# A two-layer trunk on one core: small parameters laid out by partition and loaded in three transfers, the weight queue started without them

## The chip, the cores and the metric

One NeuronCore of one Trainium2 chip. The metric is the device time of one execution in microseconds; of several runs the median is taken. Times in the rows are microseconds from the start of one profiled execution, unless marked ns.

## What is computed

The reference runs two layers on x (256 tokens, 1024 channels, float32), modulated by a vector c. Cut to what matters here:

```python
c_act = silu(c)
for i in range(2):
    mod = c_act @ ada_w[i] + ada_b[i]                  # 6144 numbers: shift, scale, gate, twice
    h = rmsnorm(x, norm_g[i, 0]) * (1 + scale_m) + shift_m
    y = s5_mixer(h, ...) if i == 0 else stick_breaking_attention(h, ...)
    x = x + gate_m * rmsnorm(y, norm_g[i, 1])
    h = rmsnorm(x, norm_g[i, 2]) * (1 + scale_f) + shift_f
    y = swiglu(h, ...) if i == 0 else moe_swiglu(h, ...)   # 8 experts, top 2
    x = x + gate_f * rmsnorm(y, norm_g[i, 3])

# s5_mixer, per group of 16 channels with a complex state of 64:
u = h @ w_in; step = exp(log_step)
lb = exp((lam_re + i lam_im) * step)                   # decay of the state
bb = (lb - 1) / lam * (b_re + i b_im)
state = scan(lb, bb u); y = re((c_re + i c_im) state) + d_skip * u
out = split(gelu(y) @ w_out): val * sigmoid(gate)
```

## The kernel before

The program is written out by hand for each engine, in one block; engines meet at semaphores only. Big weights (`ada_w`, `s5_w_in`, `s5_w_out`, the feed-forward and expert weights) come in pieces of 2 MB, 128 partitions by 4096 float32, into a ring of seven buffers. SP issues all of them (`load`, L532) in a fixed order of places: place n lies in buffer n mod 7, a load waits until the product on the buffer's last content has counted up `used`, and its landing counts up `landed`. The first places are four pieces of `ada_w[0]` (0 to 3), `s5_w_in` (4), four more of `ada_w[0]` (7 to 10), and the two halves of `s5_w_out` (11, 12). Buffers 5 and 6 hold `bs` and `wv`, small matrices that the kernel makes for the S5 layer, until places 12 and 13. At the start SP waits for `params_in` to reach 16 times 13 (L543), which is the landing of 13 parameter transfers; after that it issues pieces 0 and 1, piece 2 behind the landing of 0, piece 3 behind that of 1, and `s5_w_in` behind that of 2 (L544 to L549).

ACT's queue issues everything small (L724 to L739): c, both lambdas, log_step, d, norm_g and ada_b as rows (7 transfers), x (1 MB), the four parts of b, the two of c_re and c_im (4 and 2 transfers, with runs of 64 and 256 bytes), then the router's weights and bias. Only behind these 16 issues do ACT's own instructions follow: the squares of x (`pre_stats`, L748), Silu of c (L842), two sines, four copies of blocks of the identity (L847), four evictions of the transposed c (L853), then the evictions of the modulation (`ada_part` L779, `ada_mod` L784) and of `wv` (L793), and a part of hT (L757).

DVE waits for the 13 transfers (L1495), spreads log_step (L1496), and lets PE transpose the rows into columns (L2222, 17 transposes, and 32 matmuls for c_re and c_im, L2287). It copies them out of PSUM (L1498, L1499) and begins a long chain of small instructions on 128 x 16 elements, each waiting for the one before: `exp_small` (L1369 to L1380), c32, which is Silu(c) repeated for the product (L1505), angles, `to_hT` (x times its inverse norm, L1386), powers of the decay, then `bs` in four wide steps (L1483 to L1487, `complex_blocks`), `hT_evict` (L1394), the tables of angles (L1454 to L1463), and `resp`.

PE waits for c32 and for pieces 0 and 1 for the first product (`ada(0)`, L2248, 32 matmuls), transposes x (L2267), folds (L2258), does `ada(1)` on pieces 2 and 3, folds, transposes `bs` in eight groups (L2304, groups 4 to 7 need the second half of `bs`), and then needs hT for u (L2312). After that come the chunk sums (L2334), responses, `ada(2)`, `ada(3)`, outputs (L2371, L2373), the product with `s5_w_out` (L2413), and the later layers.

GpSimd (POOL) makes the constants, sets buffer 5 to zero (L695), waits for the squares of x and makes the two inverse norms (`inverse_norm`, L655 and L656), sets `resp` (5120 columns) to zero (L697), marks buffers 5 and 6 as landed (L699), and adds `ada_b` to the modulation (`mod_bias`, L662 to L670), on which hT waits.

Of the kernel before, what the change touches and what calls it, by code (L numbers as in the profile page):

```python
# [31 lines left out]
ACT = mybir.ActivationFunctionType  # L32
AX = mybir.AxisListType

P = 128
D = 1024
KD = D // P
# [3 lines left out]
NBLK = W5 // P  # L41
HG = 16
NS = 64
TPB = 4
NT = NBLK * TPB
# [4 lines left out]
NE = 8  # L50
# [81 lines left out]

def ada_place(layer, r):

    return ADA_PLACES[layer][r]
# [7 lines left out]
def program(nc, x, c, ada_w, ada_b, norm_g, s5_w_in, s5_lambda_re, s5_lambda_im, s5_b_re, s5_b_im,  # L143
            s5_c_re, s5_c_im, s5_d, s5_log_step, s5_w_out, sb_w_qkv, sb_w_out, ffn_w_gate_up,
            ffn_w_down, moe_w_router, moe_b_router, moe_w_gate_up, moe_w_down, out):
    ctx = ExitStack()
    with ctx:
        def sb(name, shape, dt=F32):
            return ctx.enter_context(nc.sbuf_tensor(name, shape, dt))

        def sem(name):
            return ctx.enter_context(nc.semaphore(name))

        ps = ctx.enter_context(nc.psum_tensor("ps", [P, 8, 512], F32))
# [4 lines left out]
        ident = sb("ident", [P, P])  # L159
# [6 lines left out]
        cols = sb("cols", [P, 128])  # L166
        c32 = sb("c32", [P, KD, 32])
        adab = sb("adab", [P, 4, 24])
# [4 lines left out]
        wr_sb = sb("wr_sb", [P, KD, NE])  # L173
# [61 lines left out]
        c_raw = view(at_u, (2, NBLK, NS))  # L235
        b_raw = view(at_u + 2 * NBLK * NS, (2, NT, HG))
# [59 lines left out]
        params_in, x_in, router_in = sem("params_in"), sem("x_in"), sem("router_in")  # L296
        out_written, consts_done = sem("out_written"), sem("consts_done")
        cols_ready, cols_ps, cols_done, silu_c_done, gg_done = (
            sem("cols_ready"), sem("cols_ps"), sem("cols_done"), sem("silu_c_done"), sem("gg_done"))
# [10 lines left out]
        ct_ps, ct_done, bs_done, bt_ps, wv_done = (  # L310
            sem("ct_ps"), sem("ct_done"), sem("bs_done"), sem("bt_ps"), sem("wv_done"))
# [35 lines left out]
        r_c = rows[0:KD, 0:P]  # L347
        r_lam = rows[0:NT, 128:384].rearrange("p (a n) -> p a n", a=2)
        r_ls = rows[0:NT, 384:386]
        r_lsb = rows[0:NT, 512:640].rearrange("p (a n) -> p a n", a=2)  # L350
        r_d = junk[0:NBLK, 512:640]
        r_g = tbuf[0:8, :]
        r_b = junk[0:24, 0:512]
# [6 lines left out]

        C_C, C_LRE, C_LIM, C_LS, C_D, C_G = 0, 8, 24, 40, 56, 60
# [168 lines left out]
        def _(sp):  # L530
# [12 lines left out]
            sp.wait_ge(params_in, 16 * 13)  # L543
# [80 lines left out]
        def _(pool):  # L624
# [47 lines left out]
            def router_lanes():  # L672

                pool.wait_ge(router_in, 32)
# [20 lines left out]
            pool.memset(ring[:, RING - 2, :], 0.0).then_inc(blank_done, 1)  # L695
            inverse_norm(0, ss_done, rs_done, 0, 8)
            pool.memset(resp.rearrange("p i t d h -> p (i t d h)"), 0.0).then_inc(blank_done, 1)  # L697
# [25 lines left out]
        def _(act):  # L723
            act.dma_start(r_c, c.rearrange("a (k n) -> (a k) n", n=P)).then_inc(params_in, 16)  # L724
            act.dma_start(r_lam[:, 0, :], s5_lambda_re[0].rearrange("(t g) n -> t (g n)", g=2)).then_inc(params_in, 16)
            act.dma_start(r_lam[:, 1, :], s5_lambda_im[0].rearrange("(t g) n -> t (g n)", g=2)).then_inc(params_in, 16)
            act.dma_start(r_ls, s5_log_step[0].rearrange("(t g) -> t g", g=2)).then_inc(params_in, 16)
            act.dma_start(r_d, s5_d[0].rearrange("(b g) h -> b (g h)", b=NBLK)).then_inc(params_in, 16)
            act.dma_start(r_g, norm_g.rearrange("a b n -> (a b) n")).then_inc(params_in, 16)
            act.dma_start(r_b, ada_b.rearrange("l (r n) -> (l r) n", n=512)).then_inc(params_in, 16)  # L730
            act.dma_start(x_sb[:, :, :], x[0].rearrange("(t p) d -> p t d", p=P)).then_inc(x_in, 16)
            for i, w in enumerate((s5_b_re, s5_b_im)):
                for g in range(2):
                    act.dma_start(b_raw[NS * g:NS * g + NS, i], w[0].rearrange("(t g) n h -> g n t h", g=2)[g]
                                  ).then_inc(params_in, 16)
            for i, w in enumerate((s5_c_re, s5_c_im)):
                act.dma_start(c_raw[:, i], w[0].rearrange("(b g) h n -> (g h) b n", b=NBLK)).then_inc(params_in, 16)
            act.dma_start(wr_sb[:, :, :], moe_w_router[0].rearrange("(k p) n -> p k n", p=P)).then_inc(router_in, 16)
# [100 lines left out]

            pre_stats(0)  # L840
            act.wait_ge(cols_done, 1)
            act.activation(cols[:, 0:KD], cols[:, 0:KD], ACT.Silu).then_inc(silu_c_done, 1)  # L842
# [5 lines left out]
            act.wait_ge(ct_ps, 1)  # L848
            for i in range(2):
                c_t = ps[:, 2 + i, :].rearrange("p (t g h) -> p t g h", g=2, h=HG)  # L850
                for g in range(2):
                    r = slice(NS * g, NS * g + NS)
                    act.activation(cT[r, i], c_t[r, :, g, :], ACT.Copy, scale=-1.0 if i else 1.0).then_inc(ct_done, 1)  # L853
# [495 lines left out]
        def _(dve):  # L1349
            count = [0]  # L1350

            def link(ins):

                count[0] += 1
                ins.then_inc(dve_step, 1)
                dve.wait_ge(dve_step, count[0])
# [148 lines left out]
            dve.tensor_copy(c32[:, :, :], cols[:, 0:KD].unsqueeze(2).to_broadcast([P, KD, 32])).then_inc(cols_done, 1)  # L1505
# [56 lines left out]
            dve.wait_ge(blank_done, 1)  # L1562
            complex_blocks(lambda i: bs[:, i], bs_done, (QR, QI),
# [656 lines left out]
        def _(pe):  # L2220
            def columns(dst, src, n):
                return pe.transpose(dst, src, ident[0:n, 0:n])  # L2222
# [4 lines left out]
            columns(ps[:, 0, C_LRE:C_LRE + NT], r_lam[:, 0, :], NT)  # L2227
            columns(ps[:, 0, C_LIM:C_LIM + NT], r_lam[:, 1, :], NT)
            columns(ps[:, 0, C_LS:C_LS + NT], rows[0:NT, 512:640], NT)
            columns(ps[:, 0, C_D:C_D + NBLK], r_d, NBLK)  # L2230
            for k in range(KD):
                ins = columns(ps[:, 0, C_G + 8 * k:C_G + 8 * k + 8], r_g[:, P * k:P * k + P], 8)
            ins.then_inc(cols_ps, 1)
            for j in range(4):
                ins = columns(ps[:, 1, 24 * j:24 * j + 24], r_b[:, P * j:P * j + P], 24)
            ins.then_inc(cols_ps, 1)
# [47 lines left out]
            for i in range(2):  # L2284
                for b in range(NBLK):
                    for g in range(2):
# [977 lines left out]
_INS = ["x", "c", "ada_w", "ada_b", "norm_g", "s5_w_in", "s5_lambda_re", "s5_lambda_im", "s5_b_re", "s5_b_im",  # L3264
        "s5_c_re", "s5_c_im", "s5_d", "s5_log_step", "s5_w_out", "sb_w_qkv", "sb_w_out", "ffn_w_gate_up",
        "ffn_w_down", "moe_w_router", "moe_b_router", "moe_w_gate_up", "moe_w_down"]
# [17 lines left out]
```

## Time and profile before

| What | Value |
|---|---|
| Median of 3 runs | 1480.8 us (1478.76 to 1483.89) |
| Profiled execution, its own time | 1483.81 us |
| Its span in the trace | 1482.0 us |
| Busy: PE / DVE / ACT / POOL | 1338.5 / 661.2 / 514.1 / 41.1 us |
| Moved by DMA | 474.30 MB, 320 GB/s on the mean |
| Mean granted clock of PE | 0.969 |

The span is what the trace covers; the time of the execution holds 1.8 us more. PE is busy for 90% of the span, but that is a mean over stages with different limits. In the views below "idle before <- releaser" is the time for which an engine stood before an instruction and what ended it; PEclk is the granted clock as a share of 2.4 GHz; the DMA share is the mean share of time for which the 16 DMA engines were occupied. The queue q1 holds SP's transfers, q10 ACT's.

### The profile page before, as it was taken

The page shows a single profiled execution, that of the slowest core. Times are in us where ns is not written, and L with a number is a line of the kernel's source. Part 1 is how long each engine was busy: PE and PEld are TensorE (multiplying, and loading weights), DVE is VectorE, ACT ScalarE, POOL GpSimd, SP SyncE. Part 2 cuts the span into 40 slices and gives each one's busy share as a digit, 9 for nine tenths or more (in the row PEclk, how much of TensorE's full clock was granted, in tenths as well). Part 3 has the DMA queues.
Part 4 walks back from the last instruction along what each step waited for, and adds up shares of the span by engine and source line. Part 5 has one row for each costly group of instructions (what it writes and reads, how often), then busy time and mean ns, then how long its engine had stood idle before and what let it go on. Part 6 is the DMA issues. An engine that isn't in the chain of part 4 may idle for free.

```text
span 1482.0 us, 25306 instructions
## 1 busy us (share of the span) xinstructions
PE 1338.5 (90%) x11159; PEld 956.7 (65%) x11160; DVE 661.2 (45%) x741; ACT 514.1 (35%) x563; POOL 41.1 (3%) x80
## 2 busy tenths in 40 slices
PE   3899899999999898999999999999988888987776
PEld 2674578888779645677775777776766665643332
DVE  5953354454453525555553755553864544000002
ACT  2323433434254514344442444443544441000001
POOL 3000000000010003000000000000000000000000
PEclk8989999999999998999999999999999999999999
DMA  8874794555484314799999989999999999999994
GB/s 283 331 283 153 286 412 172 179 206 183 170 341 171 114 57 170 285 341 387 412 411 412 389 335 380 410 412 412 411 411 410 409 412 412 409 413 412 412 412 181
DMA packets 206792, 474.30 MB, mean 320 GB/s; under 512 B 9986, under 2 KB 10030, under 8 KB 206670
## 3 DMA queue, kind: packets, MB, share of 16 engines
q1 hardware_dynamic: 199968, 470.83, 82.1%
q10 hardware_dynamic: 6702, 1.71, 0.5%
q8 instruction: 93, 1.52, 0.4%
q14 instruction: 29, 0.24, 0.0%
HBM read 471.47 MB, written 1.05 MB: 319 GB/s over the span
## 4 chain that ended last, share of the span: by engine, by line
PE 66%; SPq 14%; DMA 13%; DVE 3%; ACT 2%; issue 1%; ACTq 1%; POOL 1%; POOLq 0%; DVEq 0%
PE ps L2437 39%; SPq L534 14%; DMA ring<-in_moe_w_down_dram 9%; PE ps L2768 6%; PE ps L2780 4%; DMA ring<-in_ada_w_dram 3%; PE ps L2610 2%; PE ps L2413 2%; PE ps L2248 1%; DMA ring<-in_moe_w_gate_up_dram 1%; PE ps L2689 1%; PE ps L2312 1%; DVE ring_lo L1983 1%; PE ps L2373 1%; PE ps L2334 0%
## 5 line engine op out<-in xcount | busy, mean ns | idle before, releaser
L1983 DVE TENSOR_TENSOR ring_lo<-ring,w 128x2048 fp32r<-128x2048 f32 x122 | 278.9, 2289 | 177.4 <-ACT w L1118 140.3
L1118 ACT ACTIVATE w<-ring 128x2048 fp32r<-128x2048 f32 x122 | 232.9, 1912 | 205.5 <-PE ps L2437 201.8
L2768 PE MATMUL ps<-ring,arena 128*32 128x128 f32 (+1 forms) x5376 | 241.6, 293 | 33.6 <-DMA ring<-in_moe_w_gate_up_dram 22.7
L2768 PEld LDWEIGHTS ps<-ring,arena 128*32 128x32 f32 (+1 forms) x5376 | 184.6, 114 | 94.5 <-issue 36.5
L2437 PE MATMUL ps<-ring_lo,x_hi 128*128 128x512 f32 x576 | 224.7, 390 | 0.0
L1613 DVE TENSOR_TENSOR ring_lo<-ring,w_hi 128x2048 fp32r<-128x2048 f32 x42 | 95.6, 2290 | 88.5 <-ACT w_hi L837 88.5
L2437 PE MATMUL ps<-w,x_hi 128*128 128x512 f32 x320 | 128.8, 403 | 1.4 <-DVE arena L1935 1.1
L2437 PE MATMUL ps<-w,x_lo 128*128 128x512 f32 x320 | 124.9, 390 | 0.0
L2437 PEld LDWEIGHTS ps<-ring_lo,x_hi 128*128 128x128 f32 x576 | 108.3, 188 | 20.7
L2780 PE MATMUL ps<-ring,tri 128*32 128x512 f32 (+1 forms) x448 | 71.5, 652 | 34.5 <-DMA ring<-in_moe_w_down_dram 32.6
L837 ACT ACTIVATE w_hi<-ring 128x2048 fp32r<-128x2048 f32 x42 | 78.8, 1909 | 48.5 <-PE ps L2437 42.1
L2437 PE MATMUL ps<-w_hi,x_hi 128*128 128x512 f32 x224 | 89.4, 399 | 0.0
L2437 PE MATMUL ps<-w_hi,x_lo 128*128 128x512 f32 x224 | 87.3, 390 | 0.0
L2437 PEld LDWEIGHTS ps<-w,x_hi 128*128 128x128 f32 x320 | 60.0, 188 | 28.4 <-issue 15.1
L2437 PE MATMUL ps<-w,a_hi 128*128 128x512 f32 x168 | 68.4, 407 | 4.2 <-DVE a_lo L2003 3.3
L2437 PEld LDWEIGHTS ps<-w,x_lo 128*128 128x128 f32 x320 | 60.1, 188 | 12.9
L2437 PE MATMUL ps<-w,a_lo 128*128 128x512 f32 x168 | 66.4, 395 | 0.0
L2437 PE MATMUL ps<-ring_lo,a_hi 128*128 128x512 f32 x168 | 66.3, 395 | 0.0
L2248 PE MATMUL ps<-ring,c 128*32 128x512 f32 x384 | 50.2, 675 | 15.1 <-DMA ring<-in_ada_w_dram 15.1
L2780 PEld LDWEIGHTS ps<-ring,tri 128*32 128x32 f32 (+1 forms) x448 | 18.0, 123 | 68.2 <-DMA ring<-in_moe_w_down_dram 38.0
L2780 PE MATMUL ps<-ring,arena 128*32 128x512 f32 (+1 forms) x336 | 53.9, 605 | 6.6 <-DMA ring<-in_moe_w_down_dram 5.0
L1943 DVE TENSOR_TENSOR c<-c,ps 128x128 f32<-128x128 f32 (+1 forms) x28 | 8.8, 315 | 97.0 <-PE ps L2768 97.0
(409 smaller groups left out, 1701.5 us busy)
## 6 DMA issues: line engine op xcount, KB each, us to landing
ring<-in_moe_w_gate_up_dram SPq DMA_DIRECT2D x112, 2048.0 KB, 17.0
ring<-in_moe_w_down_dram SPq DMA_DIRECT2D x56, 2048.0 KB, 18.2
ring<-in_ada_w_dram SPq DMA_DIRECT2D x24, 2048.0 KB, 11.0
ring<-in_ffn_w_gate_up_dram SPq DMA_DIRECT2D x14, 2048.0 KB, 11.4
ring<-in_ffn_w_down_dram SPq DMA_DIRECT2D x7, 2048.0 KB, 8.0
ring<-in_sb_w_qkv_dram SPq DMA_DIRECT2D x6, 2048.0 KB, 8.4
ring<-in_s_w_out_dram SPq DMA_DIRECT2D x2, 2048.0 KB, 7.7
ring<-in_sb_w_out_dram SPq DMA_DIRECT2D x2, 2048.0 KB, 14.6
```

The costliest lines, as they stand in the source:

```text
L534: sp.dma_start(dst, src).then_inc(landed[n % RING], 16)
L837: act.activation(ff_half(w_hi[:, g % 2, :], half).bitcast(F32R), ff_half(gran(ff_place(g)), half), ACT.Copy).then_inc(whi_done, 1)
L1118: act.activation(half3(h).bitcast(F32R), ff_half(gran(pair_place(*main_granule(n))), half), ACT.Copy).then_inc(whi_done, 1 + h if h and h ...
L1613: dve.tensor_tensor(ff_half(ring_lo[(ff_place(g)) % RING][:, :], half).bitcast(F32R), w, ff_half(w_hi[:, g % 2, :], half), ALU.subtract).t ...
L1983: dve.tensor_tensor(ff_half(ring_lo[place % RING][:, :], half).bitcast(F32R), ff_half(gran(place), half), half3(h), ALU.subtract).then_inc ...
L2248: ins = pe.matmul(ps[32 * j:32 * j + 32, ada_bank(i), :], c32[:, 4 * part_k + k, :], gran8(places[r])[:, 4 * part_k + k, :], start=k == 0, ...
L2312: ins = pe.matmul(ps[:, Y_BANK + b // 2, 256 * (b % 2):256 * (b % 2) + 256], gran8(N_WIN)[:, k, P * b:P * b + P], hT[:, k, :], start=k == ...
L2413: ins = pe.matmul(ps[:, 2 * i + half, :], yT[:, k, P * tt:P * tt + P], gran4(WOUT_PLACES[half])[:, k, 512 * n:512 * n + 512], start=k == 0 ...
L2437: ins = pe.matmul(dst, stationary[a].bitcast(F32R), moving[b].bitcast(F32R), start=start and i == 0, stop=stop and i == 2)
L2610: ins = pe.matmul(ps[:, Y_BANK + 2 * tt + r, :], oT[:, k, P * tt:P * tt + P], gran8(n)[:, k, :], start=k == 0, stop=k == KD - 1)
L2768: ins = pe.matmul(dst[width * r:width * r + width, 0:cols], x[:, k, 0:width], weights[:, k, cols * r:cols * r + cols], start=k == 0, stop= ...
L2780: ins = pe.matmul(ps[width * r:width * r + width, bank, :], a[:, j, 0:width], weights[:, j, 512 * h:512 * h + 512], start=first and i == 0 ...
```

## The change

- The host lays out the parameters in two arrays. `columns` holds for each of 128 partitions its 284 numbers: c, both lambdas, log_step (repeated), d, norm_g, ada_b and the router's weights. `s5_cb` holds c and b of the S5 layer, 512 numbers for each partition and array.
- ACT's queue issues five transfers: `columns`, x, the two of `s5_cb` (counted by `cb_in`), and the router's bias.
- SP no longer waits for `params_in`.
- The transposes on PE, the copies on DVE and the four evictions of c on ACT are gone; one ACT instruction changes the sign of c_im. DVE and ACT wait for `params_in` (16) and for the constants.
- On ACT, Silu of c comes ahead of the squares of x.
- On GpSimd, the zeroing of `resp` comes ahead of `inverse_norm`.

```diff
@@ SP
-            sp.wait_ge(params_in, 16 * 13)
             for r in range(4):
@@ GpSimd
             pool.memset(ring[:, RING - 2, :], 0.0).then_inc(blank_done, 1)
+            pool.memset(resp.rearrange("p i t d h -> p (i t d h)"), 0.0).then_inc(blank_done, 1)
             inverse_norm(0, ss_done, rs_done, 0, 8)
-            pool.memset(resp.rearrange("p i t d h -> p (i t d h)"), 0.0).then_inc(blank_done, 1)
@@ ACT
-            act.dma_start(r_c, c.rearrange("a (k n) -> (a k) n", n=P)).then_inc(params_in, 16)
...
-            act.dma_start(r_b, ada_b.rearrange("l (r n) -> (l r) n", n=512)).then_inc(params_in, 16)
+            act.dma_start(small[:, :], columns).then_inc(params_in, 16)
             act.dma_start(x_sb[:, :, :], x[0].rearrange("(t p) d -> p t d", p=P)).then_inc(x_in, 16)
-            for i, w in enumerate((s5_b_re, s5_b_im)):
...
-            act.dma_start(wr_sb[:, :, :], moe_w_router[0].rearrange("(k p) n -> p k n", p=P)).then_inc(router_in, 16)
+            act.dma_start(cT.rearrange("p i t h -> p (i t h)"), s5_cb[0]).then_inc(cb_in, 16)
+            act.dma_start(b_raw.rearrange("p i t h -> p (i t h)"), s5_cb[1]).then_inc(cb_in, 16)
             act.dma_start(br_sb[:, :], moe_b_router).then_inc(router_in, 16)
...
+            act.wait_ge(params_in, 16)
+            act.wait_ge(consts_done, 5)
+            act.activation(cols[:, 0:KD], cols[:, 0:KD], ACT.Silu).then_inc(silu_c_done, 1)
             pre_stats(0)
-            act.wait_ge(cols_done, 1)
-            act.activation(cols[:, 0:KD], cols[:, 0:KD], ACT.Silu).then_inc(silu_c_done, 1)
...
-            act.wait_ge(ct_ps, 1)
-            for i in range(2):
...
+            act.wait_ge(cb_in, 32)
+            act.activation(cT[:, 1], cT[:, 1], ACT.Copy, scale=-1.0).then_inc(ct_done, 4)
@@ DVE
-            dve.wait_ge(params_in, 16 * 13)
-            dve.tensor_copy(r_lsb, r_ls.unsqueeze(2).to_broadcast([NT, 2, NS])).then_inc(cols_ready, 1)
-            dve.wait_ge(cols_ps, 2)
-            link(dve.tensor_copy(cols[:, 0:124], ps[:, 0, 0:124]))
-            dve.tensor_copy(adab[:, :, :], ps[:, 1, 0:96].rearrange("p (a b) -> p a b", a=4)).then_inc(cols_done, 1)
-            dve.wait_ge(cols_done, 1)
+            dve.wait_ge(params_in, 16)
+            dve.wait_ge(consts_done, 5)
...
             dve.wait_ge(blank_done, 1)
+            dve.wait_ge(cb_in, 32)
             complex_blocks(lambda i: bs[:, i], bs_done, (QR, QI),
@@ PE
             pe.wait_ge(consts_done, 5)
-            pe.wait_ge(cols_ready, 1)
-            columns(ps[:, 0, C_C:C_C + KD], r_c, KD)
...
-            for i in range(2):
-                for b in range(NBLK):
-                    for g in range(2):
-                        ins = pe.matmul(ps[NS * g:NS * g + NS, 2 + i, P * b:P * b + P], c_raw[:, i, b, :], ident[:, :],
-                                        start=True, stop=True, tile_position=(0, NS * g))
-            ins.then_inc(ct_ps, 1)
-            pe.wait_ge(cols_done, 1)
-            pe.wait_ge(cols_done, 2)
+            pe.wait_ge(c32_done, 1)
             ada(0)
```

## Rows read from the trace of the kernel before

**Rows 1.** The chain of waits in order of time, first 66 us: start, us, what

```profile
0.79 0.61 ACTq L724
...
13.56 0.45 SPq L534
...
14.06 12.32 DMA ring<-in_ada_w_dram
...
26.40 11.35 DMA ring<-in_ada_w_dram
...
37.88 6.16 PE ps L2248 x32
...
52.56 13.82 PE ps L2312 x64
```

**Rows 2.** Waits of SP's queue, 0 to 200 us: total, times, longest

```profile
SPq L534 <- DMA arena<-in_s_c_im_dram: 12.8, 1, 12.8
```

**Rows 3.** The chain of waits, later

```profile
144.78 0.37 SPq L534
...
969.30 14.96 DMA ring<-in_moe_w_down_dram
```

**Rows 4.** Stretches: length, then each engine's busy time, clock, DMA share, GB/s

```profile
40.00:42.00 2.00, 2.00 (x12) 0.45 (x8) 1.90 (x3) 0.00 (x0) 0.00 (x0) 0.50 1.05 410
120.00:140.00 20.00, 20.00 (x48) 8.92 (x47) 7.71 (x6) 4.92 (x6) 0.00 (x0) 1.00 0.05 11
```

**Rows 5.** Timeline of SP, 19 to 21.5 us

```profile
21.23 0.37 SPq L534 DMA_DIRECT2D ring<-in_ada_w_dram  x1
```

**Rows 6.** DMA: packets, two queues, x's landing (us, last), and two early stretches

```profile
DMA packets 206792, 474.30 MB, mean 320 GB/s; under 512 B 9986, under 2 KB 10030, under 8 KB 206670
...
q10 hardware_dynamic: 6702, 1.71, 0.5%
q8 instruction: 93, 1.52, 0.4%
...
x_sb<-in_x_dram ACTq DMA_DIRECT2D x1, 1024.0 KB, 6.2
...
2.00:14.00 12.00, 0.07 (x1) 0.11 (x2) 0.21 (x1) 1.78 (x2) 4.18 (x5) 1.00 0.66 142
6.00:8.00 2.00, 0.00 (x0) 0.00 (x0) 0.00 (x0) 0.00 (x0) 0.34 (x1) 1.00 1.02 395
```

**Rows 7.** Timeline, 0 to 50 us, POOL and DVE: start, us, instruction

```profile
2.82 3.51 POOL L695 MEMSET ring<- 128x4096 f32 x1
...
16.55 4.50 DVE L1369 TENSOR_SCALAR arena<-cols 128x16 f32<-128x16 f32 x1
16.59 4.36 POOL L697 MEMSET arena<- 128x5120 f32 x1
...
21.09 0.17 DVE L1370 TENSOR_SCALAR arena<-arena 128x16 f32<-128x16 f32 x1
...
24.02 0.29 DVE L1505 COPY c<-cols 128x256 f32<-128x256 f32 x1
...
43.15 2.47 DVE L1487 TENSOR_TENSOR ring<-junk,tbuf 64x1024 f32<-64x1024 f32 x2
...
47.17 1.90 DVE L1394 TENSOR_SCALAR hT<-ps,scale_c,modc 128x256 f32<-128x256 f32 x4 [1.56 <-POOL scale_c L670]
```

**Rows 8.** Timeline, 0 to 120 us, PE

```profile
15.83 3.48 PE L2287 MATMUL ps<-ident,arena 128*64 128x128 f32 x32
...
48.50 1.12 PE L2304 MATMUL ps<-ident,ring 128*128 128x128 f32 x8 [0.29 <-ACT ring L793]
...
87.14 3.62 PE L2248 MATMUL ps<-ring,c 128*32 128x512 f32 x32
```

**Rows 9.** Stretches, columns as in rows 4

```profile
36.00:37.80 1.80, 0.00 (x0) 0.00 (x0) 1.80 (x2) 0.00 (x0) 0.00 (x0) 0.51 1.04 404
...
97.50:111.00 13.50, 13.04 (x109) 12.24 (x108) 0.00 (x0) 2.09 (x3) 0.00 (x0) 0.50 1.05 407
```

More of the change, by code:

```diff
@@ L130 @@
 assert PER_EXPERT % RING == 0
+C_C, C_LRE, C_LIM, C_LS, C_D, C_G = 0, 8, 24, 40, 56, 60
+C_ADAB = 124
+C_ROUTER = C_ADAB + 96
+COLUMNS = C_ROUTER + KD * NE
 def ada_place(layer, r):
@@ L140, in ff_place, with program @@
     return N_FFN + g if g else N_FFN0
-def program(nc, x, c, ada_w, ada_b, norm_g, s5_w_in, s5_lambda_re, s5_lambda_im, s5_b_re, s5_b_im,
-            s5_c_re, s5_c_im, s5_d, s5_log_step, s5_w_out, sb_w_qkv, sb_w_out, ffn_w_gate_up,
-            ffn_w_down, moe_w_router, moe_b_router, moe_w_gate_up, moe_w_down, out):
+def program(nc, x, ada_w, s5_w_in, s5_w_out, sb_w_qkv, sb_w_out, ffn_w_gate_up, ffn_w_down, moe_b_router,
+            moe_w_gate_up, moe_w_down, columns, s5_cb, out):
     ctx = ExitStack()
@@ L165, in program @@
         half = sb("half", [P, 1])
-        cols = sb("cols", [P, 128])
+        small = sb("small", [P, COLUMNS])
+        cols = small[:, 0:C_ADAB]
+        adab = small[:, C_ADAB:C_ROUTER].rearrange("p (j r) -> p j r", j=4)
+        wr_sb = small[:, C_ROUTER:COLUMNS].rearrange("p (k n) -> p k n", k=KD)
         c32 = sb("c32", [P, KD, 32])
-        adab = sb("adab", [P, 4, 24])
         modc = sb("modc", [P, 2, MODS, 4])
@@ L172, in program @@
         stat = sb("stat", [P, 16])
-        wr_sb = sb("wr_sb", [P, KD, NE])
         br_sb = sb("br_sb", [1, NE])
@@ L234, in program @@
         rows = pl(640)
-        c_raw = view(at_u, (2, NBLK, NS))
-        b_raw = view(at_u + 2 * NBLK * NS, (2, NT, HG))
+        b_raw = view(at_u, (2, NT, HG))
         bs = ring[:, RING - 2, :].rearrange("p (i t d h) -> p i t d h", i=2, t=NT, d=CHUNK)
@@ L295, in program @@
         used = [sem(f"used{i}") for i in range(RING)]
-        params_in, x_in, router_in = sem("params_in"), sem("x_in"), sem("router_in")
+        params_in, cb_in, x_in, router_in = sem("params_in"), sem("cb_in"), sem("x_in"), sem("router_in")
         out_written, consts_done = sem("out_written"), sem("consts_done")
-        cols_ready, cols_ps, cols_done, silu_c_done, gg_done = (
-            sem("cols_ready"), sem("cols_ps"), sem("cols_done"), sem("silu_c_done"), sem("gg_done"))
+        c32_done, silu_c_done, gg_done = sem("c32_done"), sem("silu_c_done"), sem("gg_done")
         dve_step = sem("dve_step")
@@ L309, in program @@
         angle_done, table_done, blank_done = sem("angle_done"), sem("table_done"), sem("blank_done")
-        ct_ps, ct_done, bs_done, bt_ps, wv_done = (
-            sem("ct_ps"), sem("ct_done"), sem("bs_done"), sem("bt_ps"), sem("wv_done"))
+        ct_done, bs_done, bt_ps, wv_done = sem("ct_done"), sem("bs_done"), sem("bt_ps"), sem("wv_done")
         ur_done, up_ps, yg_done, yp_ps = sem("ur_done"), sem("up_ps"), sem("yg_done"), sem("yp_ps")
@@ L344, in program @@
         n_silu, n_act, n_tr, n_aT = sem("n_silu"), sem("n_act"), sem("n_tr"), sem("n_aT")
[L347 to L353, printed above, removed]
         def part(i):
@@ L359, in ada_bank @@
             return 2 if i == 8 else i % 2
-        C_C, C_LRE, C_LIM, C_LS, C_D, C_G = 0, 8, 24, 40, 56, 60
         (STEP, XM, THETA, KTURN, TURN, COST, SIN1, COS1, MAG, DEN, FHI, FLO,
@@ L672, in router_lanes @@
             def router_lanes():
-                pool.wait_ge(router_in, 32)
+                pool.wait_ge(params_in, 16)
+                pool.wait_ge(router_in, 16)
                 link(pool.memset(wr_wide.rearrange("p k n -> p (k n)"), 0.0))
@@ L723, in _ @@
         def _(act):
-            act.dma_start(r_c, c.rearrange("a (k n) -> (a k) n", n=P)).then_inc(params_in, 16)
[L725 to L729, printed above, removed]
-            act.dma_start(r_b, ada_b.rearrange("l (r n) -> (l r) n", n=512)).then_inc(params_in, 16)
-            act.dma_start(x_sb[:, :, :], x[0].rearrange("(t p) d -> p t d", p=P)).then_inc(x_in, 16)
-            for i, w in enumerate((s5_b_re, s5_b_im)):
-                for g in range(2):
[L734 to L737, printed above, removed]
-            act.dma_start(wr_sb[:, :, :], moe_w_router[0].rearrange("(k p) n -> p k n", p=P)).then_inc(router_in, 16)
+            act.dma_start(small[:, :], columns).then_inc(params_in, 16)
+            act.dma_start(x_sb[:, :, :], x[0].rearrange("(t p) d -> p t d", p=P)).then_inc(x_in, 16)
+            act.dma_start(cT.rearrange("p i t h -> p (i t h)"), s5_cb[0]).then_inc(cb_in, 16)
+            act.dma_start(b_raw.rearrange("p i t h -> p (i t h)"), s5_cb[1]).then_inc(cb_in, 16)
             act.dma_start(br_sb[:, :], moe_b_router).then_inc(router_in, 16)
@@ L847, in _ @@
                 act.activation(same[a:a + 32, :], ident[a:a + 32, a:a + 32], ACT.Copy).then_inc(ct_done, 1)
-            act.wait_ge(ct_ps, 1)
-            for i in range(2):
[L850 to L853, printed above, removed]
+            act.wait_ge(cb_in, 32)
+            act.activation(cT[:, 1], cT[:, 1], ACT.Copy, scale=-1.0).then_inc(ct_done, 4)
             ada_part(0)
@@ L1504, in _ @@
             dve.wait_ge(silu_c_done, 1)
-            dve.tensor_copy(c32[:, :, :], cols[:, 0:KD].unsqueeze(2).to_broadcast([P, KD, 32])).then_inc(cols_done, 1)
+            dve.tensor_copy(c32[:, :, :], cols[:, 0:KD].unsqueeze(2).to_broadcast([P, KD, 32])).then_inc(c32_done, 1)
             link(dve.tensor_tensor(pcol(THETA), lim, pcol(STEP), ALU.mult))
@@ L2220, in _ @@
         def _(pe):
-            def columns(dst, src, n):
-                return pe.transpose(dst, src, ident[0:n, 0:n])
             pe.wait_ge(consts_done, 5)
-            pe.wait_ge(cols_ready, 1)
-            columns(ps[:, 0, C_C:C_C + KD], r_c, KD)
[L2227 to L2236, printed above, removed]
             def ada(i, lo=0, hi=4):
@@ L2282, in gate_row @@
                 ins.then_inc(gg_ps, 1)
-            for i in range(2):
-                for b in range(NBLK):
-                    for g in range(2):
-                        ins = pe.matmul(ps[NS * g:NS * g + NS, 2 + i, P * b:P * b + P], c_raw[:, i, b, :], ident[:, :],
-                                        start=True, stop=True, tile_position=(0, NS * g))
-            ins.then_inc(ct_ps, 1)
-            pe.wait_ge(cols_done, 1)
-            pe.wait_ge(cols_done, 2)
+            pe.wait_ge(c32_done, 1)
             ada(0)
@@ L3261, in _, with laid_out, by_state @@
                 gate_row(3)
-_INS = ["x", "c", "ada_w", "ada_b", "norm_g", "s5_w_in", "s5_lambda_re", "s5_lambda_im", "s5_b_re", "s5_b_im",
-        "s5_c_re", "s5_c_im", "s5_d", "s5_log_step", "s5_w_out", "sb_w_qkv", "sb_w_out", "ffn_w_gate_up",
-        "ffn_w_down", "moe_w_router", "moe_b_router", "moe_w_gate_up", "moe_w_down"]
+_INS = ["x", "ada_w", "s5_w_in", "s5_w_out", "sb_w_qkv", "sb_w_out", "ffn_w_gate_up", "ffn_w_down", "moe_b_router",
+        "moe_w_gate_up", "moe_w_down", "columns", "s5_cb"]
+def laid_out(inputs):
+    import numpy as np
+    def by_state(a):
+        return a.reshape(NT, 2 * NS).T
+    lam = [by_state(inputs[f"s5_lambda_{part}"][0]) for part in ("re", "im")]
+    log_step = by_state(np.repeat(inputs["s5_log_step"][0][:, None], NS, axis=1))
+    skip = inputs["s5_d"][0].reshape(NBLK, P).T
+    gains = inputs["norm_g"].reshape(8, KD, P).transpose(2, 1, 0).reshape(P, 8 * KD)
+    bias = inputs["ada_b"].reshape(24, 4, P).transpose(2, 1, 0).reshape(P, 96)
+    router = inputs["moe_w_router"][0].reshape(KD, P, NE).transpose(1, 0, 2).reshape(P, KD * NE)
+    columns = np.concatenate([inputs["c"].reshape(KD, P).T, *lam, log_step, skip, gains, bias, router], axis=1)
+    c = [inputs[f"s5_c_{part}"][0].reshape(NT, 2, HG, NS).transpose(1, 3, 0, 2) for part in ("re", "im")]
+    b = [inputs[f"s5_b_{part}"][0].reshape(NT, 2, NS, HG).transpose(1, 2, 0, 3) for part in ("re", "im")]
+    s5_cb = np.stack([np.concatenate([w.reshape(P, NT * HG) for w in pair], axis=1) for pair in (c, b)])
+    return {**inputs, "columns": columns, "s5_cb": s5_cb}
 def kernel(**inputs):
@@ L3275 @@
     arrays, args = {}, []
+    inputs = laid_out(inputs)
     for name in _INS:
```

## The prediction

> **What bounds the kernel now.** I read the page first (span 1482.0 us), then the chain of waits in order of time, because this change touches only the first 50 us. The reader is to see there that the kernel begins with one long wait. The chain starts in ACT's queue, which issues small transfers one after another, goes to the landing of the last of them, and only then to SP's first weight load at 13.56 us [rows 1, 2]. From there two waits for pairs of `ada_w` loads, 12.32 and 11.35 us, and 6.16 us of matmuls on the second pair lead to the stage on hT, which keeps PE busy from 52.56 us on [rows 1]. SP's own waits name the cause: 12.8 us for the last small parameter, `s5_c_im` [rows 2].
>
> Does a gain at the start reach the end? Behind the first stages the chain is PE, then SP's issue behind PE at 144.78 us and a load, and from about 969 us on mostly loads of `w_down` and their issue [rows 3]. The weight queue is not at its limit all the time: between 120 and 140 us the DMA moved 11 GB/s, since all slots were full [rows 4]. So each later load is released by a matmul, no event is tied to absolute time, and a shift of PE at 52 us is a shift of the end.
>
> **Weight stream.** SP's wait goes. Its first load can be issued when ACT issues its first transfer, 0.79 us [rows 1], 12.77 us earlier. The loads go two at first and then each behind the landing of the one two before: issued at 13.56, 21.23 and 26.40, the first landing 7.67 us after issue, the next pair at 26.38, the fourth at 37.74 [rows 1, 5]. That is 12.82 us from first issue to two landed and 24.18 us to four. But in before these loads had the DMA engines nearly alone. Now ACT's transfers share them: columns 128 x 284 x 4 = 0.15 MB, x 1.05 MB, s5_cb 2 x 128 x 512 x 4 = 0.52 MB, together 1.72 MB, as the ACT queue's 1.71 MB of now [rows 6]. At the 410 GB/s of a full stretch [rows 4] they take 4.2 us. Two loads land at 0.79 + 12.82 + 4.2 = 17.8 us, four at 0.79 + 24.18 + 4.2 = 29.2 us, against 37.74 now: **8.6 us earlier**. Bounds of the sharing: below, nothing, if the 1.72 MB fill gaps of the weight queue; that gives 12.8 us. Above, the time for which the engines were occupied by the same queue before the weights began: a mean share of 0.66 from 2 to 14 us [rows 6], 7.9 us in all, which gives 4.9 us. I take 4.2, since the many tiny packets (9986 under 512 B [rows 6]) are what made that stretch slow, 142 GB/s on the mean against 395 GB/s at full share while x moved [rows 6], and they go; the new rows are 1 to 4 KB long.
>
> **DVE's chain.** Now it starts at 13.56 and its first `exp_small` instruction (L1369), 16 columns wide, took 4.50 us, where L1370, of the same size, takes 0.17: it ended 0.1 us behind GpSimd's memset of `resp`, 4.36 us [rows 7]. The memset moves in POOL's queue ahead of `inverse_norm`: 2.82 + 3.51 + 4.36 = 10.7 us [rows 7]. So DVE, if its columns are there at 5 or 6 us, is held until 10.8, against 21.05 now: 10.2 us earlier. Behind that instruction the chain is solid work to the second half of `bs` at 45.62 [rows 7]; it would end at 35.4. PE first wants that half in the third batch of transposes, at 48.50 [rows 8], which comes 8.6 us earlier, at 39.9. DVE's gain is larger than PE's, so DVE stays hidden. Without cover (DVE less than 5.7 us earlier, that is 8.6 less the 2.9 of slack) it would bound. c32 is ready at 24.31 - 10.2 = 14.1 us, ahead of the weights at 17.8.
>
> **What else moves or goes.** POOL's queue: the two norm results for x now stand behind the memset; x lands 6.2 us after issue now [rows 6], with half the engines' time perhaps by 11 us, so two squares and norms (some 3 us) are done by 14; DVE comes to them only behind c32 (14.1) and some dozen small instructions. Zero, with about 2 us of cover. ACT: 16 issues become 5, so its queue is free some 9 us earlier; Silu comes before the squares and waits only for columns; four evictions of cT become one, all while ACT waits for PE's product anyway. PE loses 17 small transposes and 32 matmuls on c_raw, the latter 3.48 us from 15.83 on [rows 8], after which it sat idle until the weights landed at 26.4: zero. Three small copies on DVE lie ahead of the held instruction: already counted. Router data now comes with the columns and is used after 500 us: zero.
>
> **Sum.** 8.6 us, from the fourth load's landing. Against the profiled execution (1483.8 us) that makes 1475.2; that execution stands 3.0 us above the median of the three runs, 1480.8 (1478.8 to 1483.9), so the forecast for a median is 1480.8 - 8.6 = **1472.2 us**. What this kernel's measurement can tell from no change is about 0.3%, 4.4 us.
>
> **Rivals.**
> *A, the second product runs at the full clock.* Before the second pair landed PE stood idle, the granted clock fell to 0.51 of 2.4 GHz, that is 1.2 GHz, between 36 and 37.8 us [rows 9], and its 32 matmuls took 6.16 us [rows 1], where the same 32 at 2.4 GHz took 3.62 [rows 8]. In the new order PE would have ada(0) until about 23 to 24, transposes 2 us, a fold 1 us, and wait 2 to 4 us for 29.2. If the clock is kept, another 2.5 us come: 11.1 in all, 1469.7 us. DVE would just allow it (free at 35.4, and wanted for hT at 47.17 - 11.1 = 36.1 [rows 7]). Against it: the gap is hardly shorter than now. Chance 0.22, with it the cases in which the small transfers cost nearly nothing. The Trainium skill, "TensorE: Matmul & The Clock Gate", Part 1, says that the lower clock is the default and that sustained activity releases it. By that rule ada(0), PE's first work, would begin at 1.2 GHz; the trace does not agree for the first work: 32 matmuls, among the first of all, took 3.48 us, 0.11 us each, no slower than the transposes of `bs` later, 8 in 1.12 us [rows 8]. By the rule ada(0) would end near 24 us, by the trace near 21; both are ahead of 29.2, so the sum stands by either, and only the gap that A needs short is 3 us longer by the trace.
>
> *B, the small transfers cost as much as now.* 7.9 us of engines instead of 4.2: gain 4.9, 1475.9 us. For it: the shares above [rows 6]. Against it: the tiny packets are gone. Chance 0.16.
>
> *C, the columns starve behind the weights.* In before the columns had the engines first. If the ACT queue is served only where SP's is empty, columns wait for five loads (four `ada_w` and `s5_w_in`, which SP issues without any product): 0.79 + 24.18 + 5.1 = 30.1 us (5.1 is 2.1 MB at 410 GB/s). DVE's first instruction then ends 9.2 us later than its 21.05; less 2.9 of slack at the transposes, PE comes 6.3 us late: 1487.1 us, slower. The point from which it decides is a landing of the columns at 23.5 us; between 19.5 and 23.5 there is no measurable change, and up to about 15 the forecast stands. Against it: the engines' code came over a queue of its own (93 packets [rows 6]) through stretches of 410 GB/s, so queues do share. The Trainium skill, "DMA: Bandwidth & Descriptors", Queues, rings and completion order, says that each engine takes the queues by turns, packet by packet. By that rule the columns land within some 6 us and this rival falls away; nothing in this trace shows SP's and ACT's data side by side at length. Chance 0.12, of which 0.04 slower and 0.08 the same.
>
> *Clock later on.* From 97.5 to 111 us the clock was 0.50 although PE was busy for 13.04 of 13.50 us [rows 9]. If that stretch shifts against the work it costs or gives a part of some 6 us; I take 2 either way into the range and nothing into the sum.
>
> **Chances.** Forecast 0.50 (7.4 to 9.8 us), A 0.22, B 0.16, C 0.12. Likeliest case alone: 1470.5 to 1474. Range for 8 in 10: from 1468 (A and a lucky clock) to 1477 (B and 1 us). Faster by over 0.3% takes the forecast, A, and nearly all of B: 0.85. Within 0.3%: 0.11. Slower: 0.04.
>
> **What the profile after would show.** SP's first issue before 1 us; first product of PE near 18 us, second near 29; DVE's first `exp_small` instruction or the one behind it held to 10.7; u's product starting near 44 instead of 52.4; the same clock and DMA shares behind it, and the start of the tail at 969 us shifted by as much. The forecast is wrong if PE's first product waits for DVE (c32), if the second product waits behind PE itself, or if hT is late by DVE; then a wait on DVE takes the place of the load.

## The result, and the profile after

| | before | after |
|---|---|---|
| Median, first comparison | 1483.9 us (7 executions) | 1466.0 us (7 executions, 1461.9 to 1473.8) |
| Ratio, 95% interval | | 0.9902 [0.9881, 0.9922] |
| Two more comparisons of the same two kernels | 1482.8, 1483.1 | 1471.8, 1472.9; ratios 0.9932 [0.9907, 0.9957], 0.9919 [0.9892, 0.9946] |
| Profiled execution, span | 1482.0 | 1464.2 |
| Mean granted clock of PE | 0.969 | 0.979 |

Over all 19 executions of the changed kernel the median is 1471.6 us, some 11 below that of before (1482.8 over the 66 executions beside it and the experiments). Three executions of these kernels with a clock of 0.80 or less (1646.6 us and more) were disturbed and are left out throughout. The forecast, 8.6 us faster, had the direction and the greater part. The profiled pair is 17.8 us apart, and the first reading has to split these: not all of them belong to the change.

The chain of waits of the changed kernel in order of time (start, us, what); it answers to [rows 1] and [rows 3]:

```profile
0.78 0.45 SPq L528
...
1.28 16.43 DMA ring<-in_ada_w_dram
...
17.72 10.59 DMA ring<-in_ada_w_dram
...
28.44 5.18 PE ps L2210 x32
...
42.00 13.81 PE ps L2267 x64
...
87.48 0.45 PE ps L2328 x4
...
95.09 7.13 PE ps L2368 x16
...
128.14 0.37 SPq L528
```

And two more lines of the same view of the kernel before, from the outputs stage and the product behind it:

```profile
98.44 0.85 PE ps L2373 x4
...
111.73 7.13 PE ps L2413 x16
```

Read them as differences. SP issues at 0.78 us instead of 13.56. The fourth load lands at 28.31 (17.72 + 10.59) instead of 37.74: 9.4 us. The second product takes 5.18 us instead of 6.16, and the stage on hT starts 10.6 us earlier (42.00 against 52.56). Up to here the change is at work. Then the same four matmuls of `outputs(1)` take 0.45 us instead of 0.85, and the product with `s5_w_out` starts 16.6 us earlier (95.09 against 111.73): 6.1 us more, on instructions that the change doesn't touch. SP's issue behind that product is still 16.6 us earlier (128.14 against 144.78). One more product that met a lower clock in before (5.34 us against 3.64) makes it 18.3; behind that the distance moves between 15.4 and 18.8 us and ends at 17.8, which I did not follow further.

DMA of the changed kernel, from the view of its queues (q10 is ACT's: packets, MB, share) and issues (last figure: us to landing); it answers to [rows 6]:

```profile
DMA packets 200795, 474.29 MB, mean 324 GB/s; under 512 B 3682, under 2 KB 3810, under 8 KB 200674
...
q10 hardware_dynamic: 706, 1.72, 0.3%
...
x_sb<-in_x_dram ACTq DMA_DIRECT2D x1, 1024.0 KB, 8.7
...
arena<-in_s_cb_dram ACTq DMA_DIRECT2D x2, 256.0 KB, 10.1
small<-in_columns_dram ACTq DMA_DIRECT2D x1, 142.0 KB, 3.1
```

One stretch of it, columns as in rows 4:

```profile
2.00:10.00 8.00, 0.00 (x0) 0.00 (x0) 6.12 (x2) 1.50 (x3) 7.85 (x6) 1.00 1.00 374
```

The same 1.7 MB come over ACT's queue in 706 packets instead of 6702 (of the 9986 packets under 512 B only some 6300 were ACT's small ones, as 3682 stay); the columns are there 3.1 us after their issue, beside two weight loads in flight, and from 2 to 10 us the engines moved 374 GB/s where they moved 142 from 2 to 14 us before.

Timeline of GpSimd and DVE in the changed kernel (start, us, instruction); it answers to [rows 7]:

```profile
2.83 3.51 POOL L689 MEMSET ring<- 128x4096 f32 x1
...
3.85 2.52 DVE L1349 TENSOR_SCALAR arena<-small 128x16 f32<-128x16 f32 x1 [3.74 <-DMA small<-in_columns_dram]
...
6.27 4.40 POOL L690 MEMSET arena<- 128x5120 f32 x1
6.40 4.30 DVE L1350 TENSOR_SCALAR arena<-arena 128x16 f32<-128x16 f32 x1
...
10.73 0.17 DVE L1351 TENSOR_SCALAR arena<-arena 128x16 f32<-128x16 f32 x1
...
13.47 0.29 DVE L1481 COPY c<-small 128x256 f32<-128x256 f32 x1
...
36.75 1.90 DVE L1374 TENSOR_SCALAR hT<-ps,scale_c,modc 128x256 f32<-128x256 f32 x4 [1.68 <-POOL scale_c L663]
```

DVE has its columns at 3.85 us, and two instructions of 16 columns are held, one by each memset, until 6.37 and 10.70. c32 is ready at 13.8, four microseconds ahead of the weights, and before hT DVE still waits 1.68 us (1.56 before). It is hidden, as forecast.

### The profile page after: what moved, and what is told of

It reads as the page before. It is cut to its first block, busy times and chain, and to the rows that moved or that the text cites. A ratio compares the mean times of both kernels' runs of the same rounds, so it can differ in the third digit from the quotient of the medians.

```text
span 1464.2 us, 25193 instructions
## 1 busy us (share of the span) xinstructions
PE 1328.0 (91%) x11110; PEld 946.9 (65%) x11111; DVE 662.4 (45%) x738; ACT 510.8 (35%) x559; POOL 40.7 (3%) x80
## 2 busy tenths in 40 slices
DMA packets 200795, 474.29 MB, mean 324 GB/s; under 512 B 3682, under 2 KB 3810, under 8 KB 200674
## 4 chain that ended last, share of the span: by engine, by line
PE 67%; SPq 14%; DMA 13%; DVE 3%; ACT 2%; issue 1%; POOL 1%; POOLq 0%; DVEq 0%; ACTq 0%
PE ps L2392 40%; SPq L528 14%; DMA ring<-in_moe_w_down_dram 9%; PE ps L2723 6%; PE ps L2735 4%; DMA ring<-in_ada_w_dram 3%; PE ps L2565 2%; PE ps L2368 2%; PE ps L2210 1%; DMA ring<-in_moe_w_gate_up_dram 1%; PE ps L2644 1%; PE ps L2267 1%; DVE ring_lo L1960 1%; PE ps L2493 1%; PE ps L2633 1%
## 6 DMA issues: line engine op xcount, KB each, us to landing
ring<-in_moe_w_down_dram SPq DMA_DIRECT2D x56, 2048.0 KB, 18.3
```

## The experiments

Each kernel was run beside the kernel before on one chip; the figure behind a time is the ratio to it with its 95% interval. "Clock" is the mean granted clock of one execution.

**e1, e2 and e10: the two kernels again.** No edit. They ask whether the 6.1 us in the outputs stage belong to the change.

> The kernel before once more, unchanged, to see the granted clock of each of its executions beside its time. Theory P (the stretch of low clock in the outputs stage at 97 to 111 us is a matter of phase, there in some executions and not in others): executions fall in groups some 6 to 7 us apart, with mean clocks some 0.005 apart, as the seven of the changed kernel did (0.979 to 0.980 for 1461.9 to 1466.0 us, 0.974 to 0.975 for 1470.8 to 1473.8). Rival S (the stretch belongs to the old order): all executions near 0.969, in one group within 3 us.

> The changed kernel once more, unchanged. Theory P: two groups again, some 7 us apart, near 1466 and 1473 us, with mean clocks of 0.979 and 0.974; ratio to before 0.987 to 0.993. Rival S: all executions but one or two near 1466 us with a clock of 0.979.

> The changed kernel once more on the chip of the two beside it, for the comparison: median 1466 to 1474 us, mean clocks from 0.971 to 0.980, ratio to before 0.990 to 0.993.

Measured: the kernel before 1482.5 us over 12 executions, clocks 0.969 to 0.974, in one broad group (1478.9 to 1485.4), so neither two groups nor a narrow one. The changed kernel 1471.8 and 1472.9 us, clocks 0.971 to 0.980: rival S, with nearly all executions near 1466 us, fell. Of its 19 executions in all, 6 have a clock of 0.977 or more and take 1461.9 to 1466.5 us, on the mean 1464.8; the other 13 take 1468.6 to 1474.0, on the mean 1472.5, so the two kinds nearly touch. The profile of e2 shows how it stands in the stages (the chain of waits):

```profile
28.46 3.70 PE ps L2210 x32
...
40.53 13.82 PE ps L2267 x64
...
100.06 7.13 PE ps L2368 x16
```

Here the second product ran at the full pace (3.70 us) and hT's stage started at 40.5 us, yet the product with `s5_w_out` comes at 100.06, 5.0 us later than in the first profile: the low clock is back in the outputs stage. So the same kernel has it in some executions and lacks it in others, and the 6.1 us of the first pair can't be put down to the change. Of the twelve profiles of this document without the extra matmuls of e9 and e12, eleven have the low clock in this stage and only the first one of the changed kernel lacks it. One thing stays open: none of the 71 executions of the kernel before with a recorded clock has 0.976 or more, and all three of its profiles (before, e1, e5) have the low clock there, so the change may have made the high kind more frequent. The median of the first comparison was helped by it (four of its seven executions had the high clock). Of the second product the three profiles of the changed kernel show 5.18, 3.70 and 5.40 us, those of the old order (before, e1, e5) 6.16, 5.20 and 3.70.

**e3: only SP's wait is taken out of the kernel before.** Is the wait all that stood in the way? Only this line goes:

```diff
-            sp.wait_ge(params_in, 16 * 13)
```

> The kernel before with nothing changed but SP's wait for the 13 small transfers taken out. Theory Q (SP's and ACT's queues are served by turns, a packet each, so that thousands of packets of 64 to 256 bytes wait behind packets of 2 KB): the last small parameter lands beyond 25 us, DVE starts that late, and the kernel is as slow as before or up to 15 us slower, though the weights land near 30 us. Rival B (the two queues share by bytes or by engine time, 7.9 us for the small ones): the last small parameter lands by 18 us, the fourth weight load by 33 us, and 4 to 6 us are won.

Measured: 1498.0 us, 1.0108 [1.0075, 1.0140], **slower** than before. The timeline of ACT's queue and DVE in e3:

```profile
4.32 5.28 ACTq L733 DMA_DIRECT2D arena<-in_s_b_re_dram  x2
9.63 11.06 ACTq L733 DMA_DIRECT2D arena<-in_s_b_im_dram  x2
20.73 5.55 ACTq L736 DMA_DIRECT2D arena<-in_s_c_re_dram  x1
...
35.20 0.21 DVE L1495 COPY arena<-arena 16x128 f32<-16x128 f32 x1 [35.09 <-DMA arena<-in_s_c_im_dram]
```

then from its view of issues, and one stretch of it:

```profile
x_sb<-in_x_dram ACTq DMA_DIRECT2D x1, 1024.0 KB, 9.0
```

```profile
14.00:26.00 12.00, 0.00 (x0) 0.00 (x0) 0.00 (x0) 0.00 (x0) 0.00 (x0) 1.00 1.10 381
```

The engines moved 381 GB/s while the parts of b crawled: issuing the first two took ACT 5.28 us instead of 1.44 before, the next two 11.06 instead of 4.17, c_re 5.55 instead of 0.68, and the last parameter landed at 35.1 us instead of 13.5. The 1024 KB of x, in large packets on the same queue, landed 9.0 us after issue, about as in the changed kernel (8.7): it is the small packets that starve and not the queue. Theory Q holds in its main point; by turns of one packet each is its reading, which no view here shows packet by packet. This is what rival C of the prediction feared, in a kernel that keeps the small packets. So the packing is what allows the weight stream to start early. (The packing also makes fewer transfers, 16 to 5; no run has the one without the other.)

**e4: the changed kernel, weights behind the small transfers.** It takes the overlap out and leaves the packing.

```diff
+            sp.wait_ge(params_in, 16)
+            sp.wait_ge(x_in, 16)
+            sp.wait_ge(cb_in, 32)
             for r in range(4):
```

> The changed kernel, but SP waits for columns, x and both parts of s5_cb before its first load. If the start of the weight stream carries the gain: small transfers land near 8.5 us, four loads at 8.5 + 24.2 = 32.7 us instead of 28.3, and the kernel is 4 to 5 us slower than the changed one, 5 to 7 us faster than before apart from the clock in the outputs stage. If the packing of the parameters and the shorter chain on DVE carry it and the overlap does not: within 1.5 us of the changed kernel.

Measured: 1474.4 us, 0.9935 [0.9915, 0.9956]. The chain of waits of e4:

```profile
2.19 5.37 DMA arena<-in_s_cb_dram
...
8.16 12.50 DMA ring<-in_ada_w_dram
...
20.67 10.53 DMA ring<-in_ada_w_dram
...
43.42 13.81 PE ps L2270 x64
```

The small transfers are in at 7.56, a microsecond ahead of the estimate, the fourth load lands at 31.20, 2.9 us behind the changed kernel's, and the medians are 2.8 us apart (1474.4 against 1471.6), less than the 4 to 5 expected. The intervals of the ratios overlap, so the time alone doesn't settle it; the landing does. From SP's issue at 7.66 to the fourth landing are 23.5 us alone, and 27.5 in the changed kernel beside the small ones: sharing costs 4.0 us, and starting 6.9 us earlier pays for it. Two thirds of the 9.4 us come with the packing (6.5, of which 5.9 are the earlier issue and 0.6 a shorter time from issue to the fourth landing), one third from the overlap (2.9). The order of this split matters: the overlap without the packing is e3, and it loses.

**e5 and e6: where the zeroing of resp stands.** In e5 it is moved ahead in the kernel before, in e6 moved back in the changed one.

```diff
-            inverse_norm(0, ss_done, rs_done, 0, 8)
             pool.memset(resp.rearrange("p i t d h -> p (i t d h)"), 0.0).then_inc(blank_done, 1)
+            inverse_norm(0, ss_done, rs_done, 0, 8)
```

> The kernel before with one part of the change alone: the zeroing of resp ahead of the norm on GpSimd. The first exp_small instruction on DVE falls from 4.50 to 0.17 us and DVE's chain runs 4.3 us earlier. If DVE is hidden behind the weights, as the prediction has it, PE's stage on hT starts where it did (51.5 to 52.6 us) and the time is that of before within 0.2%. Rival: DVE shares the path, and 2 to 4 us are won.

> The changed kernel with the zeroing of resp put back behind the norm. The prediction's reason (the fourth load sets the pace, DVE has slack) gives no difference: DVE runs on at 6.4 us, is held once more for 4.4 us at about 12.6, when the norms are done, and is where it was after that; 1466 to 1474 us. Rival: the hold falls on a place that matters and costs 1 to 4 us.

Measured: e5 1481.4 us, 0.9996 [0.9984, 1.0008]; e6 1473.1 us over six executions, 0.9925 [0.9900, 0.9951]. Timelines of e5 and then of e6:

```profile
15.97 0.17 DVE L1369 TENSOR_SCALAR arena<-cols 128x16 f32<-128x16 f32 x1
```

```profile
13.68 4.37 POOL L691 MEMSET arena<- 128x5120 f32 x1
13.77 4.89 DVE L1366 TENSOR_SCALAR hn<-x_sb,stat 128x1024 f32<-128x1024 f32 x1 [0.75 <-POOL stat L649]
```

In e5 the held instruction falls from 4.50 to 0.17 us, and the time stays: DVE was hidden. PE's stage on hT started at 49.49 us, ahead of the 51.5 to 52.6 expected, but the fourth load landed 0.6 us earlier there and the second product took 3.70 us instead of 6.16, which is all of it; DVE has no part in it. In e6 the hold only moves to `to_hT`, about where it was expected, and the kernel is not told apart from the changed one. This part of the change is worth nothing measurable in either order.

**e7 and e11: the first two products by halves.** Once the fourth load was seen to set the pace, PE could do half of each product on the piece that is there.

```diff
-                    for n in places:
+                    for n in places[:1] if i < 2 else places:
                         wait_landed(pe, n)
...
-                for k in range(lo, hi):
-                    for j in range(4):
+                for k, j in ([(k, 2 * r + h) for r in range(2) for k in range(4) for h in range(2)] if i < 2 else
+                             [(k, j) for k in range(lo, hi) for j in range(4)]):
+                    if i < 2 and (k, j) == (0, 2):
+                        wait_landed(pe, places[1])
```

> The changed kernel, but the first two products on ada_w take their first half (16 matmuls on the first of the two pieces) as soon as that piece has landed, and only the other half waits for the second. Theory: PE works at about 12 and at 23 us instead of idling, only 16 matmuls are left when the fourth load lands, 3.5 us at 2.4 GHz, and the clock has had work before them: PE's stage on hT starts near 40.3 us always, where the changed kernel had 42.0 in one profile and 40.5 in the other, so 0 to 1.7 us are won. Rival: with two columns of the array in use instead of four the halves take as long as the whole, and a cold second half takes 5 us or more: nothing is won or 1 us lost.

> The products by halves once more (1468.2 us in six executions). If halves pay as their profile shows (hT stage at 40.7 us whatever the clock did), the median is 1 to 3 us below that of the unchanged kernel beside it; if not, within 1 us of it.

Measured: 1468.2 and 1471.0 us, 0.9903 [0.9877, 0.9929] and 0.9913 [0.9888, 0.9938]. The chain of waits of e7:

```profile
28.71 3.65 PE ps L2213 x16
...
40.74 13.81 PE ps L2270 x64
```

After the landing 16 matmuls take 3.65 us, and hT's stage starts at 40.7 in both profiles (41.35 in e12, which has the same halves, so not quite "always"). But 32 matmuls at the full pace take 3.70, so halving the work left halves nothing, as the rival said; its other half, a cold second half of 5 us or more, did not come, and all that is won is that the clock is up. e11 came out 1.9 us below the changed kernel beside it (1472.9), inside the 1 to 3 expected; but over 12 executions the median is 1469.8 against 1471.6, which these numbers don't separate.

**e8: outputs(0) ahead of ada(3).** Does a wide product between the two runs of narrow matmuls hold the clock?

```diff
-            ada(3)
             outputs(0)
+            ada(3)
             ada_fold(3)
```

> The changed kernel with outputs(0) ahead of ada(3) on PE instead of behind it, so that the two runs of narrow matmuls (64 columns, 5.4 us each) have 32 wide ones between them. Theory N (the clock falls behind a long run of narrow matmuls, and where it falls is a matter of phase): the stretch of low clock in the outputs stage becomes rarer, most executions have a mean clock of 0.977 or more, and the median is 2 to 5 us below that of the changed kernel (1468 over its 13 executions). Rival: the clock falls as often, and the time is within 1 us of the changed kernel, or worse by up to 2 us if outputs(0) has to wait for DVE or ACT.

Measured: 1472.8 us, 0.9942 [0.9923, 0.9961], clocks 0.971 to 0.976 in nine executions, none at 0.977 or more. Its profile has the low clock again, behind the wide product. Theory N in this form failed. The rival's figure holds (1.2 us above the changed kernel).

**e9: wide matmuls among the narrow ones.** Their result is read by nobody.

```diff
                                         state[i][:, t, 0:NC - 1], start=False, stop=i == 1)
+                    if t % 2 == 0:
+                        pe.matmul(ps[:, 0, :], ident[:, :], x_sb[:, 0, 0:512], start=True, stop=True)
```

> The changed kernel with eight matmuls of 512 columns that nobody reads, one ahead of every second step of outputs(0) and outputs(1): 8 x 0.45 = 3.6 us more work on PE. Theory N (narrow matmuls in a row let the clock fall): the stretch of low clock in the outputs stage goes from nearly all executions, mean clocks rise to 0.977 or more, and the 5 to 6 us that it cost come back: 1 to 3 us faster than the changed kernel's 1470.8 (median of 13 executions so far). Theory P alone (only the phase decides, what PE runs there does not): the clock falls as often and the kernel is 3 to 5 us slower.

Measured: 1472.0 us, 0.9917 [0.9897, 0.9936]; clocks 0.978 to 0.981 in all five executions, which lie within 3.6 us. A stretch of e9 over the outputs stage, and a piece of its chain:

```profile
79.00:96.00 17.00, 17.00 (x120) 12.46 (x110) 5.04 (x8) 2.65 (x4) 0.00 (x0) 1.00 1.05 409
```

```profile
81.58 0.92 PE ps L2332 x2
```

The same stage of e2, without them:

```profile
82.00:99.00 17.00, 16.86 (x140) 16.12 (x139) 0.68 (x1) 2.52 (x5) 0.00 (x0) 0.60 1.05 408
```

PE is busy all through both stretches; the clock is 1.00 in the one and 0.60 in the other. With 6 high clocks in 19 for the changed kernel, five in a row by luck have a chance of 0.3% ((6/19)^5). So what PE runs there decides, and not the phase alone. What in it does, the columns of the wide matmuls or only that fewer narrow ones stand in a row, is not separated. The price was mis-sized: 0.87 us each (0.92 in the chain) instead of 0.45, since such a float32 matmul is two instructions (x2), 7 us in all, which eats the gain: neither the 1 to 3 us faster nor the 3 to 5 slower came true.

**e12: the same with 256 columns, on top of e7.** The diff is e7's and e9's with `ps[:, 0, 0:256]` and `x_sb[:, 0, 0:256]`.

> The products by halves and eight unread matmuls again, but of 256 columns instead of 512. In the run with 512 each cost 0.87 us (a float32 matmul is two instructions of 0.45 us), 7 us in all, and the clock stayed up in each of five executions; with 256 they should cost 3.5 us. If half the columns still hold the clock: mean clocks of 0.978 or more in all executions, and 1464 (the executions of the changed kernel without the stretch) + 3.5 - 0.5 = 1467 us, some 4 below the changed kernel's median of 1471.5. If they don't: clocks from 0.971 to 0.98 again and a median of 1473 to 1475.

Measured: **1466.1 us**, 0.9888 [0.9866, 0.9910], four executions from 1464.8 to 1469.4 with clocks 0.979 to 0.981. The stretch and the chain:

```profile
79.00:96.00 17.00, 17.00 (x148) 15.34 (x144) 3.98 (x7) 2.90 (x5) 0.00 (x0) 1.00 1.05 407
```

```profile
81.33 0.49 PE ps L2335 x2
```

As expected in both figures, 0.49 us each and the clock up. It is the fastest of the versions by its median, 5.5 us below the changed kernel's 1471.6 and 3.7 below the halves alone (1469.8); its executions lie within 4.6 us, those of the changed kernel within 12.1. It has four executions only, and the intervals of the ratios still overlap, so it is likely faster than the changed kernel, and clearly than the one before.

## Why the prediction was right, and where it was off

- **Weight stream.** Right in mechanism, a little short in size. Two loads landed at 17.7 us (forecast 17.8), four at 28.3 (29.2). The sharing was taken at 4.2 us and measures 4.0. What was mis-sized is the interval between the second and the fourth landing: I carried over 11.35 us from the one profile of before, and in the profiles after it is 10.5 to 11.1. The gain up to there is 9.4 us in the first pair and not 8.6. A pair is one draw here too: the fourth load lands at 37.7, 37.3 and 37.1 us in the old order (before, e1, e5) and at 28.3, 28.3 and 28.8 in the changed kernel (first profile, e2, e10), on the mean 8.9 us apart, so the forecast was nearer than the pair says.
- **DVE's chain.** Right: held until 10.7 us, c32 at 13.8 (14.1), hidden; e5 has c32 4.9 us earlier, 0.6 of it from earlier parameters, and nothing follows. I had the two memsets hold one instruction; they hold two, one each, with the same end.
- **Rival A.** Its premise was seen (3.70 us for the second product in e2), but in the old order too (3.70 in e5). It is no property of the new order, and the forecast of one clock for this product was one draw out of several.
- **Rival B** fell: 4.0 us and not 7.9. **Rival C** fell for this change, since the columns land 3.1 us after issue, and came true in e3. What decides it is the packets (6702 small ones, 706 large ones) and not their bytes, the same 1.7 MB.
- **The step that failed** is "Clock later on". I took 2 us either way for the stretch of low clock in the outputs stage and put it down to a shift against the work. Nothing shifted: it is there or not, whatever the change does, and costs 6.1 us in the first pair (from hT's stage to the product with `s5_w_out`, 59.2 us against 53.1; 56.3 in e5, so its length varies). With the other clock-dependent places the two kinds of execution lie 7.8 us apart. That is what took the first median, 1466.0, 2 us below my range, while the two repeats, 1471.8 and 1472.9, stand on the forecast of 1472.2. That agreement flatters: the kernel before came out at 1482.8 and not at 1480.8, so the gain is 11 us and not 8.6. 8.9 to 9.4 of them are the landing; the other 2 would be the clock, which I did not separate from chance.
- **The clock of PE's first work.** I held against the Trainium skill ("TensorE: Matmul & The Clock Gate", Part 1: the lower clock is the default, activity releases it) that the first matmuls ran at full speed, by comparing 32 matmuls on c_raw with the transposes of `bs`. These are different forms (weights of 64 columns against 128, [rows 8]), so their times could not decide it. Stretches of the changed kernel, then of the first product in the kernel before:

```profile
17.80:20.00 2.20, 2.16 (x12) 0.68 (x16) 1.85 (x11) 0.00 (x0) 0.00 (x0) 1.00 1.05 409
...
21.20:23.00 1.80, 1.80 (x20) 0.41 (x12) 1.66 (x17) 0.00 (x0) 0.00 (x0) 1.00 1.05 410
```

```profile
26.50:28.50 2.00, 1.99 (x12) 0.66 (x16) 1.91 (x6) 1.85 (x9) 0.00 (x0) 0.50 1.05 410
30.00:31.50 1.50, 1.50 (x17) 0.37 (x10) 1.26 (x9) 0.00 (x0) 0.00 (x0) 1.00 1.05 407
```

The record of the changed kernel says 1.00 in both, but 12 records of matmuls lie in the first 2.2 us and 20 in the later 1.8, and the whole product took 5.29 us where 3.6 is the full pace. In the kernel before the same product has the same two paces, 12 records in 2.0 us at a recorded 0.50 and 17 in 1.5 us at 1.00. By that rule, the trace agrees: PE began at the lower pace. The record seems to start at 1.00 and only to tell changes, so the first reading of it, before PE has worked, says nothing. The sum did not hang on it, as the product ended at 23.1, ahead of the fourth load.

## What to carry to other kernels

A queue of weights that waits for small parameters is worth starting at once, but only when the small ones are few packets: count packets, not bytes, before two queues share the engines. A wait that seems to be the loss may protect something; taking it out alone (e3) cost 15 us, although the loads it held back came earlier. And where two profiles differ on instructions that the change doesn't touch, look at the granted clock there and repeat the kernel before giving the difference to the change.

## What the runs showed of the hardware that was not expected

- With another queue full of 2 KB packets (e3), transfers of 64 to 256 byte packets took until 35.1 us instead of 13.5, and ACT needed up to 5.5 us to issue one of them, although the bytes are a few hundred KB; 1024 KB of x on the same queue took 9.0 us.
- PE can be busy without a pause and lose its clock: matmuls of 64 columns, each with weights of 128 columns, had a granted clock of 0.50 to 0.60; one of 512 columns (e9) or 256 (e12) at every second step kept it at 1.00 in both profiles, and the mean clocks of all nine executions (0.978 to 0.981) fit.
- DVE's `tensor_scalar` and a GpSimd memset don't run side by side: 4.30 us for an instruction of 0.17 us in the changed kernel, and 4.89 in e6 for one that took 0.75 just before it. In the kernel before the record has DVE's instruction starting 0.04 us ahead of the memset, and it still ended 0.1 us behind the memset.
